# A two-block transformer kernel on one core: four edits taken together in the opening, the attention stages and the final norm

## The chip, the core and the metric

The kernel runs on one core of a Trainium2 chip. The core has TensorE (PE) for matrix products, VectorE (DVE) and ScalarE (ACT) for everything elementwise, GpSimd (POOL) and SyncE (SP), which here mostly issue DMAs. The engines run side by side and are ordered by semaphores. The metric is the device time of one execution in microseconds, lower is better.

## The reference, cut to what matters

Input are 512 tokens `x` and 256 memory tokens `mem`, 1024 wide, in float32. The first block has two layers, the second block two more:

```python
# first block, layer 0
mem_n = rmsnorm(mem, g_mem)
h = rmsnorm(x, g_mix[0])
mem_k, mem_v = split(mem_n @ w_mem_kv[0])      # likewise w_mem_kv[1] for layer 1
u, q_mem = split(h @ w_in_a[0])
v = a * sigmoid(gate)                          # a, gate = halves of u + b_glu
mix = silu(layernorm(causal_dwconv(v, w_dw_a) + b_dw_a))      # 31 taps, 768 channels
mem_o = memory_attention(q_mem, mem_k, mem_v)                 # 4 heads of 64, 256 keys
x = x + concat(mix, mem_o) @ w_out[0]
x = x + conv_ffn(rmsnorm(x, g_ffn[0]), ...)
# layer 1: forgetting attention (12 heads, masked, causal) beside memory attention with mem_k, mem_v of layer 1
# second block, layer 0: stick-breaking attention beside sparse attention (8 heads, 128 chosen keys); layer 1: differential attention
# each of its layers: x = layer_norm(ALPHA*x + (1+g_m)*mixer(...)); x = layer_norm(ALPHA*x + (1+g_f)*swiglu(...))
# the result is the last layer_norm, with gain ln_ffn_g[1] and offset ln_ffn_b[1]
```

## The kernel before, in words

**Products.** Activations lie transposed, channels on the 128 partitions and 512 tokens in a row, as 8 tiles (`xT`). A float32 product is made of three passes of a faster format: an operand is split into a high part (ScalarE writes `wH`, `hH`, `gH`) and a low part (VectorE writes `wL`, `hL`, `gL` as the difference), and TensorE adds high x high, low x high, high x low. Weights come in strips of 1024 rows x 256 columns (1 MB); SyncE loads all strips in one fixed order into two landing slots `raw` (`Strip.load`), each load waiting until the strip two before it has been split; `split_high` (ScalarE, L352) and `split_low` (VectorE, L366) of strip n+2 stand in the program beside the work on strip n. Every engine's program is a list written out by hand: a wait holds all that comes behind it on that engine.

**Opening (`Opening`, and `Conv`).** SyncE issues the four loads of `x`, then 14 loads of small vectors, then weight strips 0 and 1, then the memory tokens, then the other strips. ScalarE computes the statistics of the four token tiles, waits for the turned vectors, takes them into `cols`, splits strip 0, takes tiles 0 and 1 of the normed and turned `x` (`take_high`, L1705), splits strip 1, takes tiles 2 to 7. Then come six strips of the gated projection, one for `q_mem`, and four runs of one strip each that project the memory: K and V of layer 0, K and V of layer 1 (strips 7 to 10, 6 steps of 8 matmuls each). Beside all this VectorE runs the taps of the depthwise convolution in 86 rounds (L1954), handed out by `ROUNDS`: 4 after each of the four memory runs, and 5 left for the next stage.

**Attention stages (`Mixed`).** One unit is one pair of heads by 128 queries. In slot s of the loop TensorE makes the logits of unit s (L1335), turns the probabilities of unit s-1 by transposes (L1349), and multiplies those of unit s-2 by the values (L1370); VectorE takes the maxima (L1472 or L1475) and scales the probabilities (`scale`, L1451 to L1459); ScalarE makes the exponentials (L1428) and copies the turned probabilities out of PSUM into `probsT` (`copy_turned`, L1410), both heads in one instruction. The logits of a unit wait for the copy of the unit that had its PSUM banks before. `fill` gives products whose steps are laid between the halves of the slots up to slot `pace`. Units from `deep` on use three sets of banks and turn one slot later: units 24 to 31 of the forgetting attention (about 826 to 857 us) and all 16 of the sparse attention (1468 to 1514 us). The memory attention of layer 0 (8 units, no fill, about 172 to 206 us) carries the end of the convolution and the sums of squares for its layer norm (`ConvNorm`).

**The norm after the convolution.** `ConvGate` stands in the product with `w_out[0]`, which takes channel tiles 6 and 7 (the memory heads) first. When tile 0 is wanted, `ConvNorm.tensor` adds the last sums, waits for mean and root and spreads both over the partitions; VectorE centres and scales, ScalarE applies silu (L2008) and the product goes on.

**The end (`NormParts`, `Output`).** The last product, with `w_down`, leaves its tiles to `TakeResidual`. Then: sums of all tiles by TensorE, mean, variance, reciprocal, root (L1067), spreading, and for each of the 8 channel tiles centring and scaling on VectorE (L1121) and the offset on ScalarE (L1079); then 32 transposes (L2523) into four banks, two plain copies per token tile to `tok_out`, and 8 stores.

Of the kernel before, what the change touches and what calls it, by code (L numbers as in the profile page):

```python
# [7 lines left out]
F32 = mybir.dt.float32  # L8
F32R = mybir.dt.float32r
# [46 lines left out]
def build(nc, a, out):  # L56
    ctx = ExitStack()
    with ctx:
# [76 lines left out]
        with ExitStack() as side:  # L135
            qS = sb("qS", [P, 2, SEQ], F32, side)
            kS = sb("kS", [P, 2, SEQ], F32, side)
# [53 lines left out]
        with ExitStack() as main:  # L191
            tok_out = sb("tok_out", [P, QT, D], F32, main)
        ps = ctx.enter_context(nc.psum_tensor("ps", [P, 8, SEQ], F32))
# [45 lines left out]
        out_written = sem("out_written")  # L239
# [30 lines left out]
        max_in, turned_dve, head_out = Signal("max_in", "dve"), Signal("turned_dve", "dve"), Signal("head_out", "dve")  # L270
        stick_suffix, scored = Signal("stick_suffix", "dve"), Signal("scored", "dve")
# [23 lines left out]
        class Strip:  # L295
# [14 lines left out]
            def load(self, sp):  # L310
                to = raw[:, self.slot, 0:self.size].rearrange("p (k c) -> p k c", k=self.kt)

                sp.wait_ge(weights_low.sem, START + self.n - 1)
                for lo, hi, src in self.pieces:
                    sp.dma_start(to[:, :, lo:hi], src).then_inc(raw_landed[self.slot], 16)
# [307 lines left out]
        class TakeMemV(Take):  # L623
# [4 lines left out]
            def scalar_take(self, act, s, st):  # L628
                tile = st.tiles[0]
# [76 lines left out]
        class TakeResidual(Take):  # L706
# [32 lines left out]
            def vector_take(self, dve, s, st):  # L739
# [33 lines left out]
                if self.then == "split":  # L773
                    for tile in st.tiles:
# [5 lines left out]
                        else:  # L780
                            dve.scalar_tensor_tensor(hL[:, k, :], x, col(self.norm[0], self.norm[1] + k), mine, ALU.mult, ALU.subtract
                                                     ).then_inc(lows.sem, 1)

# [468 lines left out]
        class Mixed(Stage):  # L1252
# [6 lines left out]
            def __init__(self, pairs, sets, fill=(), pace=None, values_ready=None, apart=False, source=(hH, hL), norm=None, beside=None,  # L1259
# [3 lines left out]
                self.values_ready, self.norm, self.beside = values_ready, norm, beside  # L1263
# [10 lines left out]
                self.scaled0, self.turned0, self.tact0 = scaled.reserve(n), turned_in.reserve(n), turned_act.reserve(n)  # L1274
# [40 lines left out]
            def prob(self, t, hh):  # L1315
                u = self.buffers.index(self.banks[t])
                return tmpB[:, 2 * u + hh, :] if u < 2 else tmpA[:, hh, :]
# [4 lines left out]
            def logits(self, pe, t):  # L1322
# [3 lines left out]
                if used:  # L1326
                    pe.wait_ge(turned_act.sem, self.tact0 + used[-1] + 1)
                else:
# [15 lines left out]
            def turn(self, pe, t):  # L1344
# [5 lines left out]
                mm.then_inc(turned_in.sem, 1)  # L1350

            def value(self, pe, t):
                n, pair, qt = self.units[t]
                pe.wait_ge(turned_act.sem, self.tact0 + t + 1)
# [1479 lines left out]
```

## Time and profile before

| | us |
|---|---|
| median of 3 runs | 2620.13 (2619.55 to 2621.47) |
| the profiled execution | 2621.27 |
| its span, first to last instruction | 2619.5 |
| TensorE busy in it | 2505.2 (96%) |
| VectorE busy | 1541.1 (59%) |
| ScalarE busy | 1053.6 (40%) |

The profiled execution is one run; its own time is 1.77 us more than the span of its instructions. Busy time says how full an engine is, not what the end waits for; for that there are the chain of waits and the timelines. In a timeline row the first number is the start from the span's beginning, the second the length in us, `xN` the number of instructions merged, and the brackets give the idle time before it and who ended it.

### The profile page before, as it was taken

What the parts mean: (1) busy time and instruction counts of PE and PEld (TensorE: products, weight loads), DVE (VectorE), ACT (ScalarE), POOL (GpSimd) and SP (SyncE); (2) the same over time, 40 slices, a digit from 0 to 9 for tenths busy, and PEclk for the clock granted to TensorE, in tenths of its full rate; (3) what the DMA queues carried; (4) which work ended last, traced back from release to release, by engine and by line L of the source; (5) the groups of instructions that cost most, each with busy time, mean ns of one, the idle gap of its engine ahead of it and who ended that gap; (6) DMA issues with size and microseconds to landing.
All of it is one profiled execution on the core that took longest, in us unless ns stands there. A gap on an engine that the chain in (4) does not pass through costs nothing.

```text
span 2619.5 us, 30720 instructions
## 1 busy us (share of the span) xinstructions
PE 2505.2 (96%) x12241; PEld 1957.6 (75%) x12241; DVE 1541.1 (59%) x2301; ACT 1053.6 (40%) x1604; POOL 71.6 (3%) x145
## 2 busy tenths in 40 slices
PE   7989999999998999999999899999999989999998
PEld 5667877777865787777777578888878757888886
DVE  5986678776455477768658654333364775433325
ACT  5335323334445343333553634222254763522222
POOL 2000000000000000000000000000000000000000
PEclk9989999999999999999999999999999999999999
DMA  5122356463212346555231023333223112333321
GB/s 171 51 97 65 112 168 199 142 192 95 86 55 73 97 123 185 175 161 165 77 97 65 1 65 97 97 97 95 75 73 97 49 49 65 95 94 86 97 85 45
DMA packets 327836, 262.32 MB, mean 100 GB/s; under 512 B 13426, under 2 KB 312630, under 8 KB 327696
## 3 DMA queue, kind: packets, MB, share of 16 engines
q1 hardware_dynamic: 312256, 206.13, 26.6%
q0 software_dynamic: 15440, 54.25, 6.5%
q8 instruction: 97, 1.59, 0.3%
q14 instruction: 43, 0.35, 0.0%
HBM read 258.23 MB, written 2.12 MB: 99 GB/s over the span
## 4 chain that ended last, share of the span: by engine, by line
PE 79%; DVE 9%; ACT 5%; DVEq 4%; issue 2%; DMA 0%; SPq 0%; ACTq 0%; PEldq 0%; PEld 0%
PE ps L400 52%; PE ps L414 6%; PE ps L418 6%; PE ps L422 6%; DVE wL L366 2%; PE ps L1335 2%; DVE conv_y L1954 2%; PE ps L1349 1%; DVEq L1959 1%; PE ps L2417 1%; ACT tmpB L1428 1%; PE ps L1370 1%; ACT probsT L1410 1%; DVEq L900 1%; DVE tmpA L910 1%
## 5 line engine op out<-in xcount | busy, mean ns | idle before, releaser
L366 DVE TENSOR_TENSOR wL<-raw,wH 128x2048 fp32r<-128x2048 f32 (+1 forms) x185 | 415.3, 2245 | 127.1 <-ACT wH L352 121.4
L352 ACT ACTIVATE wH<-raw 128x2048 fp32r<-128x2048 f32 (+1 forms) x185 | 345.5, 1869 | 242.0 <-PE ps L400 101.3
L400 PE MATMUL ps<-hH,wH 128*128 128x512 f32 x1656 | 430.6, 402 | 2.8 <-DVE gate L824 1.8
L400 PE MATMUL ps<-hL,wH 128*128 128x512 f32 x1656 | 425.2, 398 | 0.0
L400 PE MATMUL ps<-hH,wL 128*128 128x512 f32 x1656 | 425.1, 398 | 0.0
L400 PEld LDWEIGHTS ps<-hH,wH 128*128 128x128 f32 x1656 | 309.1, 189 | 89.1 <-issue 14.0
L400 PEld LDWEIGHTS ps<-hH,wL 128*128 128x128 f32 x1656 | 308.9, 188 | 83.2 <-issue 10.8
L400 PEld LDWEIGHTS ps<-hL,wH 128*128 128x128 f32 x1656 | 309.6, 188 | 77.3 <-issue 4.5
L936 DVE TENSOR_TENSOR tmpB<-ps,tmpB 128x512 f32<-128x512 f32 x44 | 30.4, 691 | 231.0 <-PE ps L400 231.0
L873 ACT ACTIVATE tmpA<-ff_up,cols 128x512 f32<-128x512 f32 x88 | 67.0, 809 | 238.7 <-DVEq L900 238.7
L418 PE MATMUL ps<-gH,wL 128*128 128x512 f32 x480 | 149.1, 400 | 4.7 <-DVE wL L366 4.7
L414 PE MATMUL ps<-gH,wH 128*128 128x512 f32 x480 | 149.2, 399 | 2.9 <-ACT gH L2008 1.6
L910 DVE SCALAR_TENSOR_TENSOR tmpA<-ff_up,cols,tmpA 128x510 f32<-128x510 f32 (+1 forms) x176 | 124.3, 748 | 22.8 <-ACT tmpA L873 16.7
L1790 DVE SCALAR_TENSOR_TENSOR mod_acc<-mod_ring,silu_c,mod_acc 128x1024 f32<-128x1024 f32 x84 | 107.7, 1282 | 46.9 <-DMA mod_ring<-w_mod 44.6
L422 PE MATMUL ps<-gL,wH 128*128 128x512 f32 x480 | 134.9, 397 | 0.0
L747 DVE SCALAR_TENSOR_TENSOR xT<-ps,mod_plus,xT 128x512 f32<-128x512 f32 x64 | 47.1, 748 | 147.9 <-PE ps L422 81.1
L927 ACT ACTIVATE gH<-tmpB 128x512 fp32r<-128x512 f32 x44 | 27.8, 632 | 237.9 <-DVE tmpB L936 237.9
L400 PE MATMUL ps<-gH,wH 128*128 128x512 f32 x480 | 122.7, 396 | 0.5 <-ACT mod L1819 0.5
L400 PE MATMUL ps<-gL,wH 128*128 128x512 f32 x480 | 122.4, 395 | 0.0
L400 PE MATMUL ps<-gH,wL 128*128 128x512 f32 x480 | 122.3, 395 | 0.0
L418 PEld LDWEIGHTS ps<-gH,wL 128*128 128x128 f32 x480 | 91.1, 190 | 27.5 <-DVE wL L366 5.6
L414 PEld LDWEIGHTS ps<-gH,wH 128*128 128x128 f32 x480 | 89.6, 188 | 27.3 <-issue 2.9
(357 smaller groups left out, 3255.0 us busy)
## 6 DMA issues: line engine op xcount, KB each, us to landing
raw<-w_up SPq DMA_DIRECT2D x132, 512.0 KB, 5.3
mod_ring<-w_mod POOLq DMA_DIRECT2D x96, 512.0 KB, 4.2
raw<-w_down SPq DMA_DIRECT2D x32, 1024.0 KB, 5.4
raw<-w_gate SPq DMA_DIRECT2D x44, 512.0 KB, 4.0
raw<-w_down SPq DMA_DIRECT2D x16, 768.0 KB, 4.5
raw<-w_in_even SPq DMA_DIRECT2D x9, 1024.0 KB, 5.1
raw<-w_out SPq DMA_DIRECT2D x8, 1024.0 KB, 5.3
raw<-w_in_odd SPq DMA_DIRECT2D x16, 512.0 KB, 4.5
```

What stands on the lines that cost most here:

```text
L352: last = act.activation(wH[:, st.part, 0:st.size], raw[:, st.slot, 0:st.size], ACT.Copy)
L366: last = dve.tensor_tensor(wL[:, st.part, 0:st.size], raw[:, st.slot, 0:st.size], wH[:, st.part, 0:st.size].bitcast(F32), ALU.subtract)
L400: last = pe.matmul(dst, left, right, start=(t == 0 and k == 0), stop=(t == 2 and k == self.kt - 1))
L414: pe.matmul(dst, *operands(wH, srcH, k), start=(k == order[0]), stop=False)
L418: return pe.matmul(dst, *operands(wL, srcH, k), start=False, stop=False)
L422: return pe.matmul(dst, *operands(wH, srcL, k), start=False, stop=(k == order[-1]))
L747: dve.scalar_tensor_tensor(x, t, mod_plus[:, g:g + 1], x, ALU.mult, ALU.add).then_inc(bank_read[tile.bank].sem, 1)
L873: last = act.activation(tmpA[:, 2 * u + f, :], ff_up[:, 2 * u + f, :], ACT.Identity, bias=self.bias(s, f), scale=self.weight(2, s, f))
L910: dve.scalar_tensor_tensor(t, ff_up[:, 2 * u + f, 0:SEQ - back], self.weight(2 - back, s, f), t, ALU.mult, ALU.add)
L1335: mm = pe.matmul(ps[:, bank + hh, 0:seen], pair.q[lo:lo + DH, qt * P:qt * P + P], pair.k[lo:lo + DH, 0:seen], start=True, stop=True)
L1790: dve.scalar_tensor_tensor(mod_acc[:, :], mod_ring[:, u, :], silu_c[:, k:k + 1], mod_acc[:, :], ALU.mult, ALU.add).then_inc(mod_free[u], 1)
L1954: dve.scalar_tensor_tensor(to, conv_v[:, j, 0:SEQ - back], self.weight(j, back), to, ALU.mult, ALU.add)
```

## The change

Four edits are made together.

1. *First strip.* Weight strip 0 is issued on ScalarE's own DMA queue, as the first thing after its semaphores are set, and not on SyncE's behind `x` and the vectors. ScalarE splits strip 0 before it waits for the turned vectors.
2. *Second memory.* K and V of layer 1 are no longer projected at the end of the opening; they are the `fill` of the memory attention of layer 0 (12 steps, `pace` 6, so two in each of slots 0 to 5), on banks 0 and 1. Probabilities there lie in new buffers. The convolution has 4 rounds behind the first memory run, none behind the second, and 17 inside the slots, one or two places in a slot. The sums of `ConvNorm` go to bank 6 and are finished in slot 9, with mean and variance; its spreading of the mean comes before channel tile 7 and of the root before the low part of tile 6.
3. *Probabilities by head.* In units from `deep` on, turned probabilities are signalled, copied and released head by head, and VectorE scales before it takes the head outputs `gL`.
4. *Final norm.* `TakeLast` multiplies each residual tile with the gain as it comes (`yT`). `Output` transposes `yT` at once and adds, by one matmul with 32 rows per block, mean and offset as a correction in PSUM; the copies to `tok_out` multiply by the reciprocal root of each token. Gain and offset rows are loaded by GpSimd long before.

```diff
@@ Take of the opening, queues
-            for item in loads[0:2]:
-                item.load(sp)
+            loads[1].load(sp)
...
             start_signals(act, "act")
-
+            loads[0].load(act)
...
                 self.x_tokens.statistics(act, tmpA[:, 0:2, :].rearrange("p a n -> p (a n)"))
+                split_high(act, 0)
                 act.wait_ge(vectors_turned, 1)
                 act.activation(cols[:, 0:P], ps[:, 4, 0:P], ACT.Copy)
-                split_high(act, 0)
@@ second memory
+        mem_fill = (Run("A", 1, KD, plain(mem_w[1]), TakeByScalar(memK, MEM, 2), tokens=MEM),
+                    Run("B", 1, KD, plain(mem_w[1], MEM), TakeMemV(1), tokens=MEM))
-                          (2, 4), values_ready=made(mem_runs[1], 0, 0), beside=opening)
+                          (2, 4), mem_fill, pace=6, values_ready=made(mem_runs[1], 0, 0), source=(mH, mL), beside=opening,
+                          probs=mem_probs, turns=mem_turns)
-            ROUNDS = {0: 12, 1: 1, 2: 9, 3: 12, 4: 12, 5: 7, 6: 9, "turn": 1, "mem": 4}
+            ROUNDS = {0: 12, 1: 1, 2: 9, 3: 12, 4: 12, 5: 7, 6: 9, "turn": 1}
+            MEM_ROUNDS, BETWEEN_ROUNDS, SLOT_ROUNDS = (4, 0), (1, 1, 1, 1, 1, 1, 1, 1), (1, 1, 2, 1, 1, 1, 1, 1)
+            UP, SQUARED = {0: 0, 2: 1, 4: 2, 5: 3, 6: 4, 8: 5}, {1: 0, 3: 1, 5: 2, 6: 3, 7: 4, 9: 5}
+            MEANS = 9
@@ ConvGate
                 if k >= NCONV:
+                    if k == NCONV + 1:
+                        self.norm.spread_mean(pe)
                     self.pairs.high(pe, k)
                 else:
-                    if k == 0:
-                        self.norm.tensor(pe)
                     self.norm.gate.high(pe, k)
             def low(self, pe, k):
+                if k == NCONV:
+                    self.norm.spread_root(pe)
@@ Mixed
                 for hh in range(2):
+                    if used and t >= self.deep:
+                        pe.wait_ge(turned_act.sem, self.tact0 + 2 * used[-1] + 1 + hh)
...
-                act.wait_ge(turned_in.sem, self.turned0 + t + 1)
-                act.activation(probsT[:, t % 2, 0:heads, 0:seen], ps[:, bank:bank + heads, 0:seen], ACT.Copy).then_inc(turned_act.sem, 1)
+                for hh in range(0, heads, step):
+                    act.wait_ge(turned_in.sem, self.turned0 + 2 * t + 2 * (hh + step) // heads)
+                    act.activation(self.turns[:, t % 2, hh:hh + step, 0:seen], ps[:, bank + hh:bank + hh + step, 0:seen], ACT.Copy
+                                   ).then_inc(turned_act.sem, 2 * step // heads)
...
+                    for t in self.scaled_at[s]:
+                        if t >= self.deep:
+                            self.scale(dve, t)
                     for t in self.taken_at[s]:
...
                     for t in self.scaled_at[s]:
-                        self.scale(dve, t)
+                        if t < self.deep:
+                            self.scale(dve, t)
@@ the end: TakeLast (in s == 0 it also forms row_marks, in s == 1 affine) and Output
+                    act.activation(tmpA[:, tile.slot, :], x, ACT.Square).then_inc(squares.sem, 1)
+                    if k < KD - 1:
+                        act.activation(yT[:, k, :], x, ACT.Copy, scale=col(self.weight[0], self.weight[1] + k)).then_inc(weighted.sem, 1)
...
+            def turn(self, pe, n):
+                for k in range(4):
+                    pe.matmul(ps[:, bank, k * P:k * P + P], yT[:, 4 * h + k, t * P:t * P + P], ident[:, :], start=(k == 0), stop=True,
+                              is_transpose=True, skip_group_check=True)
+            def correct(self, pe, n):
+                pe.matmul(ps[:, self.blocks[n][0], :], moments[rows, :], affine[rows, h * 512:h * 512 + 512], start=False, stop=True,
+                          skip_group_check=True).then_inc(turned_heads.sem, 1)
...
+                self.turn(pe, 0)
+                pe.wait_ge(squares.sem, take.square0 + KD)
+                sum_quarters(pe, self.STATS, mean_of, tmpA[:, self.last_tile.slot, :], False, True).then_inc(summed.sem, 1)
+                for n in range(1, 4):
+                    self.turn(pe, n)
+                pe.wait_ge(roots.sem, self.root0 + 1)
+                pe.transpose(ps[:, self.STATS, P:2 * P], quarter_std, ident[:, :]).then_inc(std_turned.sem, 1)
+                pe.wait_ge(moments_in.sem, self.moment0 + 1)
+                for n in range(4):
+                    self.correct(pe, n)
+                for n in range(4, KD):
+                    self.turn(pe, n)
+                    self.correct(pe, n)
...
-                    act.activation(tok_out[:, t, h * 512:h * 512 + 512], ps[:, n % 4, :], ACT.Copy).then_inc(turned_act.sem, 1)
+                    act.activation(tok_out[:, t, h * 512:h * 512 + 512], ps[:, self.blocks[n][0], :], ACT.Copy, scale=rstd_col[:, t:t + 1]
+                                   ).then_inc(turned_act.sem, 1)
...
-                    dve.tensor_copy(tok_out[:, t, h * 512:h * 512 + 512], ps[:, n % 4, :]).then_inc(turned_dve.sem, 1)
+                    dve.tensor_scalar(tok_out[:, t, h * 512:h * 512 + 512], ps[:, self.blocks[n][0], :], rstd_col[:, t:t + 1], None, ALU.mult
+                                      ).then_inc(turned_dve.sem, 1)
```

## Rows read from the trace of the kernel before

**Rows 1.** Page, part 1: busy us, share of the span, instructions:
```profile
PE 2505.2 (96%) x12241; PEld 1957.6 (75%) x12241; DVE 1541.1 (59%) x2301; ACT 1053.6 (40%) x1604; POOL 71.6 (3%) x145
```

**Rows 2.** Windows: us, busy PE, PEld, DVE, ACT, POOL (instructions), clock, DMA, GB/s:
```profile
178.00:206.30 28.30, 20.51 (x201) 12.06 (x201) 16.52 (x47) 15.73 (x47) 0.00 (x0) 0.79 0.07 23
206.30:217.00 10.70, 8.02 (x50) 6.22 (x47) 5.28 (x9) 5.34 (x10) 0.00 (x0) 1.00 0.01 2
826.00:857.30 31.30, 24.37 (x218) 15.69 (x216) 18.85 (x66) 19.21 (x49) 1.08 (x2) 0.95 0.15 51
1468.00:1513.60 45.60, 36.57 (x304) 22.68 (x304) 28.83 (x116) 30.30 (x84) 0.00 (x0) 0.96 0.01 1
2596.00:2619.50 23.50, 11.12 (x97) 8.43 (x96) 15.62 (x24) 9.21 (x16) 0.00 (x0) 0.73 0.23 89
```

**Rows 3.** Timeline of SyncE's queue, first 30 us: start, us, what:
```profile
7.92 5.05 SPq L315 DMA_DIRECT2D raw<-w_in_a  x4
```

**Rows 4.** Timeline of ScalarE, first 45 us; idle time before it in brackets:
```profile
2.56 1.28 ACT L983 ACT_TABLE_LOAD   x1 [2.56 <-issue]
...
10.06 0.29 ACT L1667 ACTIVATE small<-small 128x1 f32<-128x1 f32 x1
...
15.31 1.91 ACT L352 ACTIVATE wH<-raw 128x2048 fp32r<-128x2048 f32 x1 [2.63 <-DMA raw<-w_in_a]
...
20.77 1.91 ACT L352 ACTIVATE wH<-raw 128x2048 fp32r<-128x2048 f32 x1 [2.17 <-DMA raw<-w_in_a]
```

**Rows 5.** Timeline of TensorE, 60 to 235 us:
```profile
160.35 1.12 PE L400 MATMUL ps<-mH,wH 128*128 128x256 f32 x8
...
180.81 1.11 PE L1349 MATMUL ps<-ident,tmpB 128*128 128x128 f32 x4 [6.98 <-DVE tmpB L1459]
...
206.29 1.19 PE L414 MATMUL ps<-gH,wH 128*128 128x512 f32 x4
...
216.49 1.19 PE L414 MATMUL ps<-gH,wH 128*128 128x512 f32 x4 [1.59 <-ACT gH L2008]
```

**Rows 6.** Timeline of VectorE, 40 to 240 us:
```profile
172.97 2.29 DVE L366 TENSOR_TENSOR wL<-raw,wH 128x2048 fp32r<-128x2048 f32 x1
...
190.86 1.51 DVE L1954 SCALAR_TENSOR_TENSOR conv_y<-conv_v,cols,conv_y 128x483 f32<-128x483 f32 x2
...
195.24 0.76 DVE L1472 TENSOR_REDUCE small<-ps 128x1 f32<-128x256 f32 x2 [0.38 <-PE ps L1335]
196.75 0.17 DVE L1451 RECIPROCAL small<-small 128x2 f32<-128x2 f32 x1 [0.76 <-ACT tmpB L1428]
...
197.99 0.76 DVE L1472 TENSOR_REDUCE small<-ps 128x1 f32<-128x256 f32 x2 [0.38 <-PE ps L1335]
```

**Rows 7.** Waits of TensorE, 1468 to 1513.6 us: total us, times, longest:
```profile
PE ps L1349 <- DVE tmpB L1459: 3.2, 3, 1.1
PE ps L1335 <- ACT probsT L1410: 3.0, 9, 0.5
PE ps L1349 <- DVE tmpA L1459: 2.5, 2, 1.9
```

**Rows 8.** Waits of TensorE, 830 to 857.3 us:
```profile
PE ps L1335 <- ACT probsT L1410: 1.4, 4, 0.5
```

**Rows 9.** Timeline of VectorE, 1464 to 1520 us:
```profile
1484.38 0.69 DVE L1505 TENSOR_TENSOR gL<-ps,gH 128x512 fp32r<-128x512 f32 x1
```

**Rows 10.** Chain that ended last, 2565 to 2620 us: start, us, what:
```profile
2596.05 0.76 DVE xT L747
...
2599.74 0.32 ACT rstd L1067
...
2612.38 2.69 PE ps L2523 x16
...
2615.09 0.60 ACT tok_out L2531
```

**Rows 11.** DMA issues, 2565 to 2622 us: issues, KB each, median us to landing:
```profile
out<-tok_out SPq DMA_DIRECT2D x8, 256.0 KB, 2.9
```

More of the change, by code:

```diff
@@ L626, in __init__, with scalar_tile @@
                 self.layer = layer
-            def scalar_take(self, act, s, st):
-                tile = st.tiles[0]
+            def scalar_tile(self, act, tile):
                 act.wait_ge(tile_done.sem, tile.done)
@@ L1252, in build, with __init__ @@
         class Mixed(Stage):
-            def __init__(self, pairs, sets, fill=(), pace=None, values_ready=None, apart=False, source=(hH, hL), norm=None, beside=None,
+            def __init__(self, pairs, sets, fill=(), pace=None, values_ready=None, apart=False, source=(hH, hL), norm=None, beside=None, probs=tmpB, turns=probsT,
                          deep=None, deep_sets=None, outs=None, first_use=()):
@@ L1325, in logits @@
                 used = [e for e in range(t) if self.banks[e] == bank]
-                if used:
-                    pe.wait_ge(turned_act.sem, self.tact0 + used[-1] + 1)
-                else:
+                if used and t < self.deep:
+                    pe.wait_ge(turned_act.sem, self.tact0 + 2 * used[-1] + 2)
+                if not used:
                     for signal, count in self.first_use.get(bank, ()):
@@ L1972, in __init__, with add_quarters @@
                 self.plain0 = plains.reserve(NCONV)
+            def add_quarters(self, pe, lo, src, first, final):
+                for g in range(QT):
+                    last = pe.matmul(ps[GROUP * g:GROUP * g + GROUP, self.SUMS, lo:lo + P], ones[:, 0:GROUP], src[:, g * P:g * P + P],
+                                     start=first and lo == 0, stop=final, skip_group_check=True)
+                return last
             def square(self, act, j):
@@ L2184, in vector @@
                 self.convolve(dve, self.ROUNDS[6])
-                for run in self.mem:
+                for run, rounds in zip(self.mem, self.MEM_ROUNDS):
                     split_low(dve, run.strips[0].n + 2)
-                    self.convolve(dve, self.ROUNDS["mem"])
+                    self.convolve(dve, rounds)
             def tensor_slot(self, pe, s):
-                if s < 2 * NCONV - 1:
-                    if s % 2 == 0:
-                        self.norm.sum_up(pe, s // 2)
-                    else:
-                        self.norm.sum_squares(pe, s // 2)
+                if s in self.SQUARED:
+                    self.norm.sum_squares(pe, self.SQUARED[s])
+                if s in self.UP:
+                    self.norm.sum_up(pe, self.UP[s])
             def tensor_rest(self, pe):
@@ L2526, in scalar @@
-            def scalar(self, act):
-                self.norm.scalar(act)
+                self.summed0, self.square0, self.mean0 = summed.reserve(2), squares.reserve(1), means.reserve(1)
+                self.variance0, self.root0, self.moment0 = variance_in.reserve(1), roots.reserve(1), moments_in.reserve(1)
+                self.std0, self.inverse0 = std_turned.reserve(1), inverted.reserve(1)
+                tiles = [t for st in take.run.strips for t in st.tiles]
+                self.last_tile = tiles[-1]
@@ new lines, in __init__, with load @@
+                self.blocks = [(t.bank, t) for t in tiles[2:]] + [(self.MEANS, None), (self.STATS, None)]
+            def load(self, pool, mixed):
+                pool.wait_ge(value_in.sem, mixed.value0 + len(mixed.units))
+                pool.memset(affine_rows[:, :], 0.0)
+                pool.drain()
+                for t in range(QT):
+                    for lo, name in ((GROUP * t, "ln_ffn_g_2"), (GROUP * t + 3, "ln_ffn_b_2")):
+                        pool.dma_start(affine_rows[lo:lo + 3, :], a[name][1].partition_broadcast(3)).then_inc(affine_in, 16)
@@ new lines, in turn @@
+            def turn(self, pe, n):
+                h, t = n // QT, n % QT
+                bank, tile = self.blocks[n]
+                if tile is not None:
+                    pe.wait_ge(bank_read[bank].sem, tile.read)
+                for k in range(4):
+                    pe.matmul(ps[:, bank, k * P:k * P + P], yT[:, 4 * h + k, t * P:t * P + P], ident[:, :], start=(k == 0), stop=True,
+                              is_transpose=True, skip_group_check=True)
+            def correct(self, pe, n):
+                h, t = n // QT, n % QT
+                rows = slice(GROUP * t, GROUP * t + GROUP)
+                pe.matmul(ps[:, self.blocks[n][0], :], moments[rows, :], affine[rows, h * 512:h * 512 + 512], start=False, stop=True,
+                          skip_group_check=True).then_inc(turned_heads.sem, 1)
```

229 lines of the change are left out of this document (179 added, 50 removed).

## The prediction

> **What bounds the kernel now.** I read the page first: TensorE is busy for 2505.2 us of 2619.5, so an edit elsewhere pays only where TensorE stands still or is slow [rows 1]. The windows then say how much there is to have at the four places. In the memory attention, 178 to 206.3 us, TensorE is busy 20.5 of 28.3 us, at a granted clock of 0.79; in the norm behind the convolution 8.0 of 10.7; in the deep units 24.4 of 31.3 and 36.6 of 45.6; in the tail 11.1 of 23.5 [rows 2]. Last the timelines, waits and chain at each place. The first 18 us wait for weights [rows 3, 4]; the rest of the opening is dense. Between these places TensorE works without holes, so a gain at one place moves all later work by as much, and the gains add.
>
> **First strip.** SyncE reaches the strip loads only at 7.92 us; it issues strips 0 and 1 in 5.05 us [rows 3]. ScalarE, done with the statistics of `x` at 10.35, starts to split strip 0 at 15.31 and strip 1 at 20.77, both ended by the DMA [rows 4]. After: ScalarE is free to issue at 2.56. I take about 0.43 for each of its two issues, an estimate (SyncE's four strip issues took 5.05, that is 1.26 each, which is the upper end, the queue then being full). So statistics end 0.9 later, at 11.2 (with the upper end 12.9). The strip has had 8 us to land by then, beside 2 MB of `x`, so it is split from 11.2 to 13.1. Strip 1 is now first on SyncE, at 7.92, and takes the place of strip 0: landed by 15.3, and ScalarE, after `cols` and two tiles, is free at about 15. Split 1 starts near 15.2 and not at 20.77: **-5.6**. What follows, one tile after the other behind split 1, moves with it. If `x` lands much later by sharing, the gain falls to about -3; if strip 1 lands earlier than strip 0 did, ScalarE itself limits it to -6.
>
> By the Trainium skill ("Trainium Kernel Development and Optimization", Key Constraints), DMAs of several queues run on the same 16 DMA engines, and a second queue saves only the issue time. By that rule the gain would be the time SyncE spent on issues ahead of strip 0, 7.92 less 2.56, or 5.4: the rows agree with it, and nothing more is to be had.
>
> **Second memory.** The stretch to compare runs from the first step of the second memory's K, 160.35, to the first product with `w_out`, 206.29: 45.9 us [rows 5]. In it TensorE does 12 steps, then stands for 6.98 and works slowly, since VectorE is behind with taps and splits. After: the logits may start when V of layer 0 has been copied, 0.9 after 160.35 (a copy of 0.6 and its wait, an estimate by the 0.60 copy of [rows 10]). From there VectorE bounds. Per unit it has the maxima (0.76) and the scaling; a unit's period is 2.75, from 195.24 to 197.99, with 0.76 and 0.38 idle, so 1.61 is work [rows 6]. The rest is: 22 tap instructions in 17 rounds (5 rounds of two, 12 of one) at 0.75 [rows 6], or 16.5; two splits of 2.2 [rows 6], 4.4; one `gL`, 0.7 [rows 9]. Sum 8 x 1.61 + 16.5 + 4.4 + 0.7 = 34.5. The waits inside a unit (0.76 and 0.38) are filled by the taps laid there; I add 1 for the first logits and ends that don't meet. Behind the last scaling come turn, copy, value: 2.8, about one period. Start of `w_out`: 160.35 + 0.9 + 35.5 + 2.8 = 199.6, not 206.29: **-6.7**. The 12 steps are 0.96 each (8 in 1.12 overlapped); two a slot make TensorE's slot some 4.2 us of work against 3.2 to 5.4 on VectorE, so they are mostly covered. If the cover fails in three slots the price is 3; if all 11.5 us were exposed it would be +4.8. Best case, VectorE without any stall and the taps fully in the gaps: -9. The loads of the two strips are in the same order on SyncE, and ScalarE's splits of 1.91 [rows 4] lie in slots 3 and 6, where it has room.
>
> TensorE's clock is 0.79 in this stretch [rows 2], after standing 6.98 us [rows 5]; the turn at 180.81 took 1.11 for four. With the fill it has no such hole, and I reckon with durations at 2.4 GHz. The Trainium skill ("TensorE: Matmul & The Clock Gate", Part 1: The HAM clock gate) has the same reading: throttled is the default and activity releases it. Were it to stay at 1.2 GHz the fill would not fit in the slots, and this part would give nothing.
>
> **Norm behind the convolution.** Now `w_out` starts at 206.29 and tile 0 is taken at 216.49, 10.2 later [rows 5], for 20 matmuls of some 0.23 (4.7) and a chain of mean, variance, root, spread. After: mean and root are ready at the start or within 2 us; the 20 matmuls and 16 for spreading (1.3) are 6.0, then ScalarE's silu after the spread root leaves about 1 of waiting: 7.1. **-3.1**, bounds -1 (roots late behind the last squares) and -4.2 (no waiting).
>
> **By head.** In the sparse attention TensorE waits 3.0 us in 9 waits for the copies, and 5.7 in five for scaled probabilities [rows 7]. Each wait of the first kind (about 0.31) goes when head 0's copy starts half a turn earlier and head 0's logits follow it. But three of the nine lie where the wait for scaling comes next, and are only moved: -2.0. Of the second kind, the `gL` (0.69, 0.60 apart) [rows 9] came ahead of the scaling once per four units: 4 x 0.6, -2.4. One of these holes was followed by slow matmuls (clock 0.96 [rows 2]); -0.6. Forgetting attention: 1.4 in four waits [rows 8], of which 1.2, and two `gL` of which TensorE felt 1.0: -2.2. Sum **-7.2**. ScalarE has 24 instructions more, some 0.1 each beyond what the halves save; it is busy 30.3 of 45.6 [rows 2], so this is hidden. What is late next is the chain logits, maxima, exponential, scaling, which bounds the gain; bounds -2.5 and -9.
>
> **Final norm.** Before, the last residual tile is taken at 2596.05, the root at 2599.74, and eight tiles go through VectorE and ScalarE until the last 16 transposes start at 2612.38, take 2.69, and the last copy starts at 2615.09 [rows 10]: the span ends 3.8 after that copy. After, from the same 2596.05: last sum of squares 2598.3 (0.3 later, the first turned block stands ahead); variance, root 2599.3; three small VectorE instructions, moments at 2600.4; meanwhile 12 transposes of 0.17 [rows 10]. Corrections 0 to 3 at about 0.24 (by the product of [rows 5], 1.19 for four overlapped) start at 2600.5; blocks 4 to 7 of 0.7 + 0.24 each end at 2605.2. The last copy runs 2605.2 to 2605.8, then issue and landing as before (2.9 for a store [rows 11], 3.8 in all): end at 2609.5. **-10.0**. The 2 MB of stores start near 2601.6 and are not the limit. Bounds: -11.5 (copies quicker) and -7.5 (corrections or the scaled copies 0.3 longer each, 8 in line). The added work earlier (7 copies with gain of 0.6, the affine rows, the row marks, some 6 us in all) lies on engines that wait for TensorE in this product; if it were exposed it would cost 2 at most.
>
> **The sum.** -5.6 - 6.7 - 3.1 - 7.2 - 10.0 = -32.6, against the profiled execution's 2621.27: 2588.7, say 2589. That execution lies 1.1 above the median, 2620.13, so the median would allow 2587.5; I stay with 2589.
>
> **Rivals.**
> *The attention stages are bound by their chain.* Taking waits out of TensorE only uncovers the next link; by head gives -2.5, the second memory -3. For it: VectorE's and ScalarE's waits alternate there. Against: holes of both kinds stand in the rows. Time: 2621.3 - 5.6 - 3 - 3.1 - 2.5 - 10 = 2597. Chance 0.17.
> *The strip does nothing*, since `x` is delayed by what it shares and split 1 still ends on the DMA as late as before: 2589 + 5.6 = 2594.6. For it: both splits were ended by DMAs [rows 4]. Against: the gap before 7.92. Chance 0.08.
> *Slower: the granted clock of the dense stages.* With fewer holes the core draws more; if the clock of TensorE in dense work fell, 2505.2 us busy [rows 1] stretch by their share. It decides from 1.3%: 32.6 of 2505.2. At 2%, 2589 + 50 = 2639. Against: the dense stretch at 206.3 has clock 1.00 [rows 2], and the clock falls only where TensorE stands. Chance 0.03.
> *More than reckoned*: the stages gain their upper ends, 2582: chance 0.07. The forecast itself has 0.65.
>
> **How the numbers follow.** Range 2581 to 2600: it takes in the two rivals that keep most of the gain and the better ends, and leaves out the slow clock and the case of two failures at once. A measurement here tells 0.2% (5.2 us) from no change. Slower needs the clock or an unseen stall of over 38 us: 0.03. Within 0.2% needs over 27 of the 32.6 to go: 0.01. Faster 0.96.
>
> **What would show it.** Split 1 on ScalarE at about 15 us; `w_out` at about 194 (206.29 - 5.6 - 6.7) with the clock near 1.00 between 160 and 194; tile 0 some 7 us behind it; TensorE's waits for copies in the sparse stage under 1 us in all and the stage near 40.6 long; the tail, from the last residual to the end, 13.5 and not 23.5. A step is wrong where its stretch keeps its old length. The forecast as a whole is wrong if the dense stages change length.

## The result and the profile after

The changed kernel takes **2593.46 us** (median of 4 runs, 2592.90 to 2593.99), the kernel before beside it 2619.84 us; the ratio is 0.9896, with a 95% interval of 0.9885 to 0.9908. That is 26.4 us less, where 31 were forecast (2589 against 2620.1): faster, inside the range of 2581 to 2600, and 4.5 us above the forecast. The profiled execution took 2593.99 us with a span of 2592.2.

First the page, its part on busy time and its part on the chain that ended last (shares of the span by engine):

```profile
PE 2499.6 (96%) x12218; PEld 1954.3 (75%) x12218; DVE 1532.7 (59%) x2298; ACT 1053.2 (41%) x1628; POOL 76.4 (3%) x154
...
PE 85%; DVE 6%; ACT 4%; DVEq 2%; issue 1%; DMA 0%; ACTq 0%; PEldq 0%; PEld 0%
```

TensorE is busy 5.6 us less than before [rows 1]. Of these 3.2 lie in the tail (11.12 us [rows 2], 7.96 below), which has fewer instructions and a higher granted clock; the rest goes with less work at the lower clock. From its first release to the end of the span the granted clock was at its lower level (1.2 GHz) for 56.8 us, against 84.6 before. The other 21.7 us are idle time that is gone. Then the windows of the five stretches that answer to [rows 2] (columns as there); the first is the memory attention from 160 us on:

```profile
160.00:197.90 37.90, 32.74 (x320) 23.96 (x320) 32.02 (x66) 23.16 (x56) 0.00 (x0) 0.95 0.25 84
197.90:205.30 7.40, 6.74 (x41) 5.47 (x37) 4.79 (x9) 3.35 (x8) 0.00 (x0) 1.00 0.01 3
817.00:847.60 30.60, 25.16 (x223) 16.86 (x221) 18.75 (x66) 20.27 (x57) 1.07 (x2) 0.94 0.16 52
1458.00:1498.80 40.80, 36.03 (x304) 23.08 (x304) 28.83 (x116) 31.25 (x100) 0.00 (x0) 1.00 0.01 1
2579.10:2592.20 13.10, 7.96 (x73) 4.98 (x65) 5.55 (x12) 4.00 (x8) 0.00 (x0) 0.92 0.42 160
```

The sparse stage does the same 304 matmuls in 40.8 us and not 45.6, and the tail is 13.1 us long and not 23.5. To see where each microsecond came from I lined the instructions of VectorE up, one by one, in the two traces. The difference in start, after less before:

```
opening, at 110 us of before      -0.9
memory stage and norm, at 217    -11.2   (-7.5 up to w_out, -2.8 behind it)
before the deep forgetting, 823   -8.5
behind it, 860                    -9.7
before / behind sparse            -10.0 / -14.8
last residual tile, 2596          -17.0
end of the span                   -27.3
```

### The profile page after: what moved, and what is told of

Read it like the earlier page. It is cut to its first block, busy times and chain, and to the rows that moved or that the text cites. A ratio compares the mean times of both kernels' runs of the same rounds, so it can differ in the third digit from the quotient of the medians.

```text
span 2592.2 us, 30725 instructions
## 1 busy us (share of the span) xinstructions
PE 2499.6 (96%) x12218; PEld 1954.3 (75%) x12218; DVE 1532.7 (59%) x2298; ACT 1053.2 (41%) x1628; POOL 76.4 (3%) x154
## 4 chain that ended last, share of the span: by engine, by line
PE 85%; DVE 6%; ACT 4%; DVEq 2%; issue 1%; DMA 0%; ACTq 0%; PEldq 0%; PEld 0%
PE ps L416 55%; PE ps L434 7%; PE ps L430 7%; PE ps L438 6%; PE ps L1431 2%; PE ps L2037 1%; DVE wL L382 1%; PE ps L1445 1%; PE ps L1469 1%; PE ps L2548 1%; DVEq L994 1%; DVE tmpA L1004 1%; DVEq L1006 1%; ACT tmpB L1530 1%; DVEq L1903 1%
## 5 line engine op out<-in xcount | busy, mean ns | idle before, releaser
L1004 DVE SCALAR_TENSOR_TENSOR tmpA<-ff_up,cols,tmpA 128x510 f32<-128x510 f32 (+1 forms) x176 | 124.2, 747 | 23.2 <-ACT tmpA L967 17.1
L762 DVE SCALAR_TENSOR_TENSOR xT<-ps,mod_plus,xT 128x512 f32<-128x512 f32 x56 | 41.2, 747 | 133.8 <-PE ps L438 73.0
```

Source lines behind the costliest of these rows:

```text
L762: dve.scalar_tensor_tensor(x, t, mod_plus[:, g:g + 1], x, ALU.mult, ALU.add).then_inc(bank_read[tile.bank].sem, 1)
L1004: dve.scalar_tensor_tensor(t, ff_up[:, 2 * u + f, 0:SEQ - back], self.weight(2 - back, s, f), t, ALU.mult, ALU.add)
```

## The experiments

Twelve kernels ran, in three groups of four; ratios are to the kernel before, on the same chip. Four put in one part of the change each.

**e1: the first strip alone.**

```
-            for item in loads[0:2]:
-                item.load(sp)
+            loads[1].load(sp)        # and loads[0].load(act), first on ScalarE
```

> The kernel before with edit 1 alone (strip 0 on ScalarE's queue, split 0 ahead of the vectors). Theory: the opening is limited by the bytes that the 16 DMA engines still have to move before strip 1 has landed (x, two strips, the memory tokens, small loads), not by the place in SyncE's queue. Then split 1 starts near 19.8 us instead of 20.77 and the kernel gains about 1 us. Rival (the prediction's step): the place in the queue decides, split 1 near 15.2 us, gain 5.6 us; in the joined kernel something else took it back.

Measured: 2619.82 us, ratio 0.9996 (0.9987 to 1.0005). By itself this part does nothing that can be told from no change, where 5.6 us were forecast. Split 1 (ScalarE's work on strip 1, as split 0 is on strip 0) starts at 17.58 in the trace, 3.2 earlier than in [rows 4], but only 1.5 us of it is left at 110 us. The theory had the gain about right and split 1 too late.

**e2: the second memory alone, with the norm behind the convolution** (separate `mem_probs` and `mem_turns`, K and V of layer 1 in slots between the units, mean and root early).

> The kernel before with edit 2 alone (second memory as fill, rounds of the convolution, sums and spreading of the norm behind it). Theory: VectorE bounds the stage; the stretch from the first step of layer 1's K to the first product with w_out falls from 45.9 to about 38.5 us and tile 0 follows about 7.3 us behind it instead of 10.2: in all -10.3 us, so 2609.5 us. Rival: the gain in the joined kernel came partly from a better phase of TensorE's clock, and alone it is under 7 us.

Measured: 2612.87 us, ratio 0.9967 (0.9957 to 0.9978), 8.6 us of 2620; `w_out` starts at 200.30 and tile 0 at 208.62, with an opening 0.8 us later than before: -6.8 and -8.7 against the same opening. Forecast -6.7 and -9.8. The norm is thus only 1.9 us shorter here (8.32 us from `w_out` to tile 0), for the granted clock was at its lower level until 202.4 us, 2.1 us into it.

**e3: copies by head alone**, with the scaling of the deep units put ahead of `gL`.

```
+                    if t >= self.deep:
+                        mm.then_inc(turned_in.sem, 2 // pair.heads)
```

> The kernel before with edit 3 alone (turned probabilities by head, scaling ahead of gL in the deep units). Theory: -4.9 us in the sparse attention and -1.5 in the last eight units of the forgetting attention, so about -6.4 and 2613.5 us. Rival: the forecast's -7.2, should the joined kernel have lost something between the stages to the phase of TensorE's clock; or under -3, if the stages are bound by the chain logits, maxima, exponential, scaling.

Measured: 2615.56 us, ratio 0.9978 (0.9967 to 0.9989), 5.8 us. In the trace the sparse stage loses 4.9 us and the deep forgetting units 1.2; forecast 5.0 and 2.2.

**e4: the final norm alone** (transposes first, moments folded in by a correcting product).

> The kernel before with edit 4 alone (final norm behind its transposes). Theory: the tail from the last residual tile to the end falls from 23.45 to about 13.2 us, nothing else moves: -10.3 us, 2609.6 us. Rival: the work added ahead (copies with the gain, affine rows, row marks, about 6 us on VectorE and ScalarE) shows in the last product and takes back 2 us.

Measured: 2610.41 us, ratio 0.9958 (0.9943 to 0.9973), 11 us. From the last residual tile (2591.72) to the end of the span (2605.4) it takes 13.7 us, against 23.45. That trace also shows something else: its start of that tile is already 4.3 us earlier than before, with identical code up to there. Between 1520 and 2290 us alone 4.8 us are won, where its clock was at the lower level for 17.1 us and not 23.9.

The four ratios times 2620 sum to 26.5 us, the joined change gave 27: within their intervals the parts add.

**e5: the memory tokens later.** On the changed kernel:

```
+            sp.wait_ge(raw_landed[1], loads[1].all_landed)   # ahead of the load of tok_mem
```

> The changed kernel, but SyncE waits until strip 1 has landed before it issues the load of the memory tokens (1 MB, which now follows strip 1 at once). Theory A (the 16 DMA engines are the limit of the opening: they are busy 0.97 of the first 18 us, so moving strip 0 to another queue only re-orders the same bytes): with 1 MB out of the way split 1 on ScalarE starts some 2.5 us earlier, near 17.3 instead of 19.80; but the tiles behind it are held by cold matmuls (two in 1.22 us), so the later work moves by 0.5 to 1.5 us, time near 2592. Rival B (the strips are late through their own issue on ScalarE and SyncE): split 1 stays at 19.5 to 20, time unchanged or 1 us worse through late memory tokens.

Measured: 2591.98 us, ratio 0.9886 (0.9873 to 0.9899). Splits at 12.77 and 17.81, and 3.1 us won at 110 us: the split came as theory A had it, the gain was twice what it allowed. But see e10, where it did not hold.

**e6: scaling ahead of takes and splits in the units that are not deep.** On the changed kernel:

```
+                    for t in self.scaled_at[s]:      # moved up from behind the loops
+                        if t < self.deep:
+                            self.scale(dve, t)
                     for tile in self.takes[s]:
                         tile.strip.run.take.vector_tile(dve, tile)
```

> The changed kernel with one step moved in all attentions that are not deep: VectorE scales the probabilities of a tile ahead of the fill's takes and split_low instead of behind them, as it already does in the deep units. Theory A (the last hole of the second memory, 2.95 us before the turn at 197, is the split_low of 2.29 us standing ahead of the scaling, and the slow matmuls behind it follow from the hole): the first product with w_out starts 3 us earlier after the opening (stretch 38.5 to about 35.5), time 2588 to 2590. Rival B (the fill's taps and splits are then late, so TensorE's fill products wait instead): stretch 38 to 39, and the differential attention gets up to 2 us longer, time 2593 to 2596.

Measured: 2612.33 us, ratio 0.9964 (0.9953 to 0.9976): 19 us slower than the changed kernel, and neither theory had said so. All of it lies in the differential attention (in VectorE's aligned instructions the difference goes from -2.8 us to +17.4 against the changed kernel between 2000 and 2140 us). The waits of ScalarE and VectorE there, 2015 to 2160 us (total us, times, longest), the changed kernel first, then e6:

```profile
ACT tmpB L1530 <- DVE small L1577: 34.8, 15, 2.9
...
DVE small L1553 <- ACT tmpB L1530: 16.2, 17, 2.6
```

```profile
ACT tmpB L1530 <- DVE small L1577: 51.6, 14, 5.5
...
DVE small L1553 <- ACT tmpB L1530: 39.5, 27, 3.7
```

The reciprocal (L1553) waits for the exponential. A reading that fits these rows, which no further run tested: with takes and splits ahead of it, that wait was covered by them; with the scaling first, VectorE stands at the head of its queue for 39.5 us and not 16.2, the takes and a split of 2.29 come after that, and the maxima for the next exponential (ScalarE's first row) come later still. In the memory stage the hole that theory A was after did shrink (2.95 to 1.38), but `w_out` starts 37.4 us behind the first logits, against 37.5 in the changed kernel. TensorE's clock was low for 6.8 us behind the hole and not 3.4; in e5, e10 and e11, which have the hole of 2.95 and 6.8 us at the lower clock, it is 37.9 or 38.0. So the shorter hole gives half a microsecond at most.

**e7: both**, e5 (and GpSimd's vector loads held as well) and e6.

> Both edits on the changed kernel: scaling ahead of takes and splits, and the memory tokens (SyncE) and the vectors that GpSimd loads issued only when strip 1 has landed. Theory A (bytes limit the opening, and order on VectorE limits the second memory): split 1 near 17, K step of the second memory 1 to 2 us earlier than 159.5, w_out near 193, time 2586 to 2589. Rival B (neither is the limit): 2593 to 2596.

Measured: 2608.33 us, ratio 0.9949 (0.9936 to 0.9962). The loss of e6 again, so both theories miss; split 1 came at 17.11, and 1.2 us was won at 110 us.

**e8: only the order.** On the kernel before, scaling ahead of `gL` in the deep units, with the turned probabilities copied in one piece:

```
+                    for t in self.scaled_at[s]:      # ahead of take_vector
+                        if t >= self.deep:
+                            self.scale(dve, t)
```

> The kernel before with only one part of the third edit: in the deep units VectorE scales ahead of the low part gL; the turned probabilities are still copied in one piece. Theory A (my split of the third edit: of 7.2 us some 2.4 in the sparse and 1.0 in the forgetting attention belong to the order of gL and scaling, the rest to the copies by head): sparse stage 45.6 to about 43, forgetting attention 1 us shorter, time 2616 to 2617. Rival B (the whole gain of the third edit, 5 to 6 us, comes from this order): sparse stage near 41, time 2614.

Measured: 2616.96 us, ratio 0.9979 (0.9970 to 0.9988). The sparse stage loses 2.8 us, as theory A had it (45.6 to 42.8), the deep forgetting units 0.3. The waits of TensorE in the sparse stage (total us, times, longest) of e8, and below of e3, which has the copies by head too:

```profile
PE ps L1340 <- ACT probsT L1415: 3.3, 10, 0.5
PE ps L1354 <- DVE tmpB L1464: 2.2, 4, 1.0
PE ps L1354 <- DVE tmpA L1464: 1.9, 2, 1.3
```

```profile
PE ps L1356 <- DVE tmpB L1472: 2.4, 4, 1.0
PE ps L1356 <- DVE tmpA L1472: 1.8, 2, 1.3
...
PE ps L1342 <- ACT probsT L1422: 0.3, 1, 0.3
```

Against [rows 7], the order alone takes the waits for scaled probabilities from 5.7 to 4.1 us and leaves those for the copies (3.0, now 3.3); the copies by head take the latter to 0.3. Each of the two edits removes a wait of its own. In the trace they are worth 2.8 and 2.1 us; the whole times of e3 and e8 can't tell the 2.1 (0.9978 and 0.9979, each to within 0.001).

**e9: TensorE kept at work in the opening.** On the changed kernel, 56 transposes of the identity, whose result nobody reads:

```
+                for _ in range(WARM):
+                    pe.transpose(ps[:, 5, 0:P], ident[:, :], ident[:, :])
                 self.columns_in(pe, [0], 4, first_vectors_in, ...)
```

> The changed kernel with 56 extra transposes of the identity matrix on TensorE ahead of its first real work (from about 4.1 us, when the constants are there, to about 12 to 13 us; their result is overwritten). They work out nothing and only keep TensorE busy while it would wait for the first vectors (14.4 us). Theory A (what swallowed the gain of the first edit is the half clock at which TensorE works behind split 0: released only at 23.2 us in the changed kernel and at 17.5 in e5_mem_late, with 3.1 and not 0.9 us won at 110 us): the clock is released before 13 us, the first 8 transposes take 1.1 instead of 1.9 us and the tiles behind splits 0 and 1 1.8 instead of 3.4, so all work from 30 us on starts 2 to 2.5 us earlier, time near 2591. Rival B (the landing of split 1's strip at 19.8 sets the rest): no more than 0.7 us earlier, time 2593. Rival C (the early transposes hold up the first vectors): up to 1 us later.

Measured: 2593.05 us, ratio 0.9894 (0.9879 to 0.9908), the same as the changed kernel: the time of rival B, though more was won in the opening than its 0.7 us. The clock was released at 8.6 us, and the eight first transposes took 1.04 and not 1.91 us. But TensorE then stood 1.32 and 1.31 us, and from 18.8 to 22.2 us the clock was at its lower level again, just behind the start of split 1 (17.83). 2.1 us was won at 110 us, within what openings without these transposes gave.

**e10: e9 and e5 together.**

> As e9_warm, and SyncE issues the load of the memory tokens only when strip 1 has landed. Theory A (clock and bytes are two separate limits of the opening): split 1 near 17.5 as in e5_mem_late, no slow products behind it, work from 30 us on 3.5 to 5 us earlier than in the kernel before (0.9 in the changed kernel, 3.1 in e5), time 2589.5 to 2591. Rival B (e5 had already all that the clock gives, its clock being released at 17.5): the same as e5, 3 us, time 2592.

Measured: 2593.89 us, ratio 0.9897 (0.9882 to 0.9912). Both theories miss. ScalarE's two splits, from the timeline of e5 and of e10, whose loads are the same:

```profile
12.77 1.91 ACT L368 ACTIVATE wH<-raw 128x2048 fp32r<-128x2048 f32 x1 [1.80 <-DMA raw<-w_in_a]
...
17.81 1.92 ACT L368 ACTIVATE wH<-raw 128x2048 fp32r<-128x2048 f32 x1 [0.77 <-DMA raw<-w_in_a]
```

```profile
15.24 1.91 ACT L369 ACTIVATE wH<-raw 128x2048 fp32r<-128x2048 f32 x1 [3.61 <-DMA raw<-w_in_a]
...
20.08 1.91 ACT L369 ACTIVATE wH<-raw 128x2048 fp32r<-128x2048 f32 x1 [1.39 <-DMA raw<-w_in_a]
```

With the same loads in the same order, the strips land 2.3 to 2.5 us apart in two executions. So the early landing in e5's trace can't be put down to the later load. The windows of e10 show more (columns as in [rows 2]):

```profile
18.60:20.07 1.47, 1.32 (x3) 0.56 (x3) 1.47 (x3) 0.09 (x1) 0.00 (x0) 0.50 0.06 18
```

In the last 1.5 us before split 1 starts, the DMA engines together are busy only 0.06 of the time. The semaphore events in the traces say what is missing then. A strip is loaded by two DMAs, and each adds 16 to the semaphore that the split waits for, in single steps. For strip 1 of e10, 31 of the 32 steps had come by 17.96 us, and the last came at 20.06. In the changed kernel it is 17.89 and 19.78, in e11 18.09 and 20.08; in e12 the last three come between 19.15 and 19.62, and in the kernel before the last five between 19.61 and 20.75, behind 18.65 for the rest. In e1, e5, e6 and e9 the last step comes at 17.55 to 17.80, at most 0.4 us behind the one before it. So whether split 1 starts near 17.7 or near 20 hangs on a small part of the strip that lands some 2 us behind the rest. What makes it late no run tells.

**e11: the changed kernel once more.**

> The changed kernel once more, on the same chip and beside the same runs as the other three, so that they can be compared with it: 2593.5 us, ratio 0.9896. Its opening gain at 110 us, 0.9 in the first profile, should come out anywhere from 0.5 to 3 if the moment at which the clock is released varies from execution to execution (e6, with the same opening, had 2.8).

Measured: 2593.70 us, ratio 0.9895 (0.9878 to 0.9911), as in the first measurement.

**e12: e10, and scaling early in the second memory alone.**

```
-                        if t >= self.deep:
+                        if t >= self.deep or self.probs is mem_probs:
```

> As e10_warm_mem_late, and VectorE scales ahead of takes and split_low in the second memory's attention alone (e6 lost 19 us with this order in the attentions filled with matrix work, and none of it in the second memory). Theory A (the hole of 2.95 us there gets 1.4 us shorter): 1 us faster than e10, near 2589. Rival B (as in e6, where the shorter hole was followed by 6.8 instead of 3.4 us at the half clock and the stage kept its length): the same as e10.

Measured: 2599.84 us, ratio 0.9918 (0.9904 to 0.9933), 6 us slower than e10. The edit did more than the expectation says: unlike e6, it puts the scaling also ahead of `gL` and of the convolution tap that VectorE does between a unit's maxima and its scaling. VectorE's waits in this stage, 158 to about 200 us, the changed kernel and then e12:

```profile
DVE small L1574 <- PE ps L1431: 0.8, 2, 0.5
```

```profile
DVE small L1554 <- ACT mem_probs L1531: 6.1, 8, 0.8
```

One tap moved by one place leaves VectorE idle for 0.76 us in each of eight units, 6.1 in all, and the stretch from 140 to 217 us is 8.3 us longer than e10's. Most of what the second memory and its norm gained (10.3 us) hangs on that tap in the gap.

## Why the prediction was right, and where it was not

**The first strip: forecast -5.6, measured -0.9** (e1: not to be told from nothing). This is the step that failed: that the place in SyncE's queue decides when the strips land. In the changed kernel the queue of ScalarE, its two splits, and the strip load of SyncE's queue read:

```profile
2.70 1.42 ACTq L331 DMA_DIRECT2D raw<-w_in_a  x2
...
14.49 1.91 ACT L368 ACTIVATE wH<-raw 128x2048 fp32r<-128x2048 f32 x1 [3.11 <-DMA raw<-w_in_a]
...
19.80 1.91 ACT L368 ACTIVATE wH<-raw 128x2048 fp32r<-128x2048 f32 x1 [1.87 <-DMA raw<-w_in_a]
```

```profile
9.10 1.02 SPq L331 DMA_DIRECT2D raw<-w_in_a  x2
...
10.16 4.82 SPq L2935 DMA_DIRECT2D tok_mem<-mem  x2
```

The strip is issued 5.2 us earlier than at 7.92 [rows 3] and split 0.8 earlier. "The strip has had 8 us to land by then" was wrong: it took up to 11.8. ScalarE's issues took 0.71 each, where I had put 0.43, a figure for which no row stands. SyncE issued strip 1 at 9.10 and not at 7.92, since its small loads ahead of it took longer, and the first vectors came at 14.4 us, where TensorE had its first in about 11.9 before. The DMA engines' share in the first 18 us went only from 0.92 to 0.97, in the windows (first before, then after):

```profile
0.00:18.00 18.00, 2.15 (x9) 1.78 (x9) 4.91 (x12) 9.87 (x18) 13.56 (x36) 1.00 0.92 262
```

```profile
0.00:18.00 18.00, 2.75 (x10) 2.28 (x11) 5.73 (x12) 10.27 (x18) 13.51 (x36) 1.00 0.97 276
```

Engines that are 0.92 busy have little left for a load that is issued earlier: `x`, two strips and the memory tokens are 5.2 MB, and at 276 GB/s that is 19 us, an estimate, whatever queue asks. It is not the whole cause: nearly all of strip 1 had landed by 17.9 us, and the last of its 32 steps came at 19.78 (see e10). The Trainium skill ("Trainium Kernel Development and Optimization", Key Constraints) says that a second issuing engine saves issue time alone; I had read that as a promise that the issue time would be saved. Here it was only the ceiling: 5.2 us of issue time went into 0.8 us at split 0.

All fourteen traces together, split 0, split 1 and the difference at 110 us, five without this part and nine with it:

```
without (before, e2, e3, e4, e8)        14.88-16.01   20.33-21.11   -0.6 to +0.8, mean +0.3
with (after, e1, e5-e7, e9-e12)         12.77-15.24   17.11-20.10   -3.1 to -0.6, mean -1.6
```

Only four of the nine (the changed kernel, e1, e6 and e11) have this opening without a further edit; their means are 18.8 for split 1 and -1.5.

So in the mean split 1 comes 2.2 us earlier and 1.8 us of it stay. What eats more in single executions goes with TensorE's clock. It was first released at 22.7 us before, at 23.2 in the changed kernel, at 17.5 in e5, and until then two products take 1.22 us and not 0.71. In e1 (split 1 at 17.58, release at 22.7) half of the 3.2 us or more are gone by 31 us; in e5 (17.81, release at 17.5) none. The Trainium skill ("TensorE: Matmul & The Clock Gate", Part 1: The HAM clock gate) says that the number of slow matmuls at the start varies between runs of one kernel; the changed kernel's opening, with releases at 20.3 (e6), 22.8 (e11) and 23.2, agrees. Split 1 starts in two groups, at 17.1 to 17.8 or at 19.6 to 20.1. In the later group one to three of the strip's last steps come some 2 us behind the others (see e10); why they do stays open, and neither the later load of the tokens nor anything else tried separates the groups.

**The second memory: forecast -6.7, measured -7.5.** The timeline of TensorE in the changed kernel:

```profile
160.46 0.70 PE L1431 MATMUL ps<-memK,q_mem 64*128 64x256 f32 x4 [0.84 <-issue]
...
194.07 1.12 PE L1445 MATMUL ps<-ident,mem_probs 128*128 128x128 f32 x4 [2.95 <-DVE mem_probs L1561]
...
197.92 1.19 PE L430 MATMUL ps<-gH,wH 128*128 128x512 f32 x4
...
205.29 0.96 PE L430 MATMUL ps<-gH,wH 128*128 128x512 f32 x3 [0.66 <-ACT gH L2124]
```

VectorE bounds the stage, as reckoned: up to its last tap it waits 0.8 us in all. From 159.46, where the step behind V of layer 0 would start (160.35 less the 0.89 of the opening), the start of `w_out` takes 38.5 us, against 45.9 [rows 5]. The 6.98 us hole with its slow turn is gone, and the clock of the stretch from 160 us on rose from 0.85 to 0.95. One hole of 2.95 us is left that I had not seen, made by VectorE's order:

```profile
190.96 2.29 DVE L382 TENSOR_TENSOR wL<-raw,wH 128x2048 fp32r<-128x2048 f32 x1
193.16 0.16 DVE L1553 RECIPROCAL small<-small 128x2 f32<-128x2 f32 x1
```

A split stands ahead of the scaling that the turn waits for. e6 and e12 tried two simple ways to turn that round: e6 won half a microsecond of the stage at most, e12 made it longer.

**The norm behind the convolution: forecast -3.1, measured -2.8.** 7.37 us from `w_out` to tile 0, against 10.2, with 0.66 of waiting left, by the rows just shown. The size owes something to luck: of the traces with this edit only this one and e9 (7.38) have the full clock in the whole stretch. In e2, e5, e6, e10 and e11, where 1.5 to 2.1 us of it are at the lower clock, it takes 8.1 to 8.3, so that 1.9 to 2.1 us are won; the five traces without the edit all have 10.2.

**By head: forecast -7.2, measured -6.1** in the two stages (sparse 4.9 of 5.0, deep forgetting 1.2 of 2.2). e8 bears out the split within the sparse stage: order 2.8 (forecast 2.4, and 0.6 for the slow matmuls behind it; the clock of the stage is now 1.00), copies 2.1 (forecast 2.0). The forgetting part was over-sized by half, and it is the order that gave nothing there: the waits for copies fell from 1.4 [rows 8] to 0.3 as reckoned, but those for the scaled probabilities stayed, 5.1 us before and 5.0 after, where 1.0 was to be won (e8 had 0.3), and the clock was 0.94 against 0.95.

**The final norm: forecast -10.0, measured -10.3.** The chain of waits of the changed kernel, to be laid beside [rows 10]:

```profile
2579.05 0.76 DVE xT L828
...
2582.00 0.32 ACT rstd L2707
...
2583.15 0.36 DVE moments L2728
2583.51 0.14 issue
2583.64 0.50 PE ps L2669 x2
...
2587.76 0.43 PE ps L2669
2588.20 0.02 issue
2588.22 0.69 ACT tok_out L2712
```

The moments are ready 4.5 us behind the residual tile (forecast 4.35), then a turned block and its correction in 1.01 us each (forecast 0.94), the last copy at +9.2 (forecast +9.2, 2605.2 less 2596.05).

**What no step had.** Between these places I had held TensorE to work without holes, so that gains would simply add. Two rows of its timeline in the kernel before say otherwise:

```profile
352.51 0.73 PE L418 MATMUL ps<-gH,wL 128*128 128x512 f32 x2 [2.38 <-DVE wL L366]
...
2134.67 0.92 PE L1335 MATMUL ps<-difK,difQ 64*128 64x384 f32 x4 [3.78 <-ACT probsT L1410]
```

Within 1.3 us of the end of each of these two waits the clock fell to its lower level, at 353.8 and 2135.6 us. The code there is the same, and yet 2.7 us were lost between 217 and 823 us and 2.2 won between 1514 and 2296. Other traces move by other amounts at the same places (e4 by 4.8 us between 1514 and 2296, with no edit before the tail). Behind the sparse attention they go with the time at the lower clock. From 1520 to 2290 us the kernel before, e2 and e3 have 23.9 us of it and differ by 0 to 1.1 us; the changed kernel and the eight others (e6 and e7, whose code differs there, left aside) have 17.1 or 20.5 us of it and are 2.1 to 4.8 us shorter. The 2.7 us are not explained so, for the changed kernel has 17.1 us at the lower clock between 218 and 820, as much as the kernel before; what lengthened that stretch stays open. The prediction named a changed length of the dense stages as the sign that it was wrong as a whole, and by this sign its premise failed. That the sum came out so near is in part luck, for here the drifts nearly cancel: -0.9 - 7.5 - 2.8 + 2.7 - 1.2 - 4.9 - 10.3, with -2.4 in the remaining stretches, is -27.3. Against the forecast sum of -32.6 the miss is 5.3, of which the first strip is 4.7. Of the rivals, "the strip does nothing" (2594.6, 0.08) was nearest to what happened: split 1 still waited for the DMA (1.87 us in the row above), though it came 1 us earlier and not as late as before; the rows for it stood in [rows 4].

No version that was run beats the changed kernel: e5, e9 and e10 lie within 1.5 us of it, which these measurements don't tell apart.

## What to carry to other kernels

Before a load is moved to a freer queue, look at the share of the DMA engines in that stretch: where it was 0.92 here, 5.2 us of earlier issue gave 0.8 us at the first strip, and a load counts as landed only with its last part, which here came up to 2.1 us behind the rest. On an engine that works through its list in order, what stands ahead of a waiting step decides how long the engine stands; the scaling moved forward was worth 2.8 us in the sparse stage, cost some 20 us in the differential attention and 8 us in the second memory when it came ahead of the tap. Whether to move it is read from the waits of both engines, stage by stage. A stage's gain is read from its own stretch in aligned traces, since whole times of unchanged code move by several microseconds with the clock.

## What the hardware showed that I had not expected

Identical loads in identical order landed up to 2.5 us apart in the first 20 us (splits at 12.77 and 17.81 in e5, 15.24 and 20.08 in e10). Keeping TensorE at work ahead of its real start released its clock at 8.6 us (e9), but two idle times of 1.3 us and thin work behind them were followed by the lower clock again at 18.8, and the whole time was the same (2593.05 against 2593.46 us). A load of 1 MB can wait some 2 us for the last of its 32 landing steps, while the 16 DMA engines together are busy 0.06 of the last 1.5 us (e10).
